# Eight groups of modulation columns summed over partitions by accumulating transfers instead of by TensorE

## The reference, cut to what matters

```python
sh_m, sc_m, gt_m, sh_f, sc_f, gt_f = [m[:, None, :] for m in
    jnp.split(jax.nn.silu(c) @ w_mod[l] + b_mod[l], N_MOD, axis=-1)]
csh_m, csc_m, ... = jnp.split(
    jax.nn.silu(c_ctx) @ w_mod[l] + b_mod[l], N_MOD, axis=-1)
h_lat = modulate(rms_norm_2(x, norm_mix_g[l]), sh_m, sc_m)
h_ctx = modulate(rms_norm_2(y, norm_mix_g[l]), csh_m, csc_m)
```

## Time and profile before

| | us |
|---|---|
| median of 3 runs | 2608.2 |
| lowest and highest | 2608.12 and 2608.32 |
| span of the profiled execution | 2606.1 |

### The profile page before, as it was taken

One profiled execution on the slowest core, in us unless ns is written; L12 is line 12 of the kernel. 1 busy time (PEld: TensorE's weight loads), 2 busy tenths in 40 slices (PEclk: granted clock), 3 DMA queues, 4 the chain that ended last, 5 costly groups with the idle time before them and its releaser, 6 DMA issues.

```text
span 2606.1 us, 35655 instructions
## 1 busy us (share of the span) xinstructions
PE 2588.4 (99%) x13302; PEld 2184.3 (84%) x13302; DVE 1841.0 (71%) x3324; ACT 1367.4 (52%) x2620; POOL 176.2 (7%) x232
## 2 busy tenths in 40 slices
PE   8999999999999999999999999999999999999999
PEld 7999889888888888888888898888788888888887
DVE  5677665677799999666877775667767665555555
ACT  5445565655545445465767565555544444444443
POOL 1011100022100000000011100000001111000000
PEclk9999999999999999999999999999999999999999
DMA  8796655589988888866787765544578887666664
GB/s 271 236 298 183 191 172 173 181 281 286 285 287 271 275 285 267 285 194 198 237 250 233 242 179 147 161 136 148 163 233 254 253 256 226 185 193 192 187 193 161
DMA packets 313724, 576.67 MB, mean 221 GB/s; under 512 B 30012, under 2 KB 38496, under 8 KB 313424
## 3 DMA queue, kind: packets, MB, share of 16 engines
q1 hardware_dynamic: 295824, 558.11, 68.1%
q0 software_dynamic: 17552, 16.22, 3.1%
q10 hardware_dynamic: 176, 0.07, 0.0%
HBM read 568.02 MB, written 2.10 MB: 219 GB/s over the span
## 4 chain that ended last, share of the span: by engine, by line
PE 97%; DVE 1%; ACT 1%; issue 0%; DMA 0%; ACTq 0%; DVEq 0%
PE ps L1825 27%; PE ps L1827 26%; PE ps L1826 26%; PE ps L1814 3%; PE ps L1815 3%; PE ps L1816 3%; PE ps L1758 2%; PE ps L1913 1%; PE ps L1883 1%; PE ps L1902 1%; DVE wlo L2465 0%; PE ps L2028 0%; DVE tl L2511 0%; PE ps L2045 0%; PE ps L2017 0%
## 5 line engine op out<-in xcount | busy, mean ns | idle before, releaser
L2465 DVE TENSOR_TENSOR wlo<-raw,whi 128x512 fp32r<-128x512 f32 x1712 | 1098.6, 687 | 525.5 <-ACT whi L2132 522.8
L2132 ACT ACTIVATE whi<-raw 128x512 fp32r<-128x512 f32 x1712 | 982.2, 624 | 808.2 <-PE ps L1827 516.6
L1825 PE MATMUL ps<-whi,th 128*128 128x512 f32 (+1 forms) x3124 | 1231.7, 394 | 2.2 <-ACT hA L2326 1.0
L1827 PE MATMUL ps<-whi,tl 128*128 128x512 f32 (+1 forms) x3124 | 1211.4, 388 | 0.0
L1826 PE MATMUL ps<-wlo,th 128*128 128x512 f32 (+1 forms) x3124 | 1210.2, 387 | 0.0
L1825 PEld LDWEIGHTS ps<-whi,th 128*128 128x128 f32 x3124 | 586.9, 188 | 122.0 <-issue 5.1
L1827 PEld LDWEIGHTS ps<-whi,tl 128*128 128x128 f32 x3124 | 586.5, 188 | 121.8
L1826 PEld LDWEIGHTS ps<-wlo,th 128*128 128x128 f32 x3124 | 587.3, 188 | 115.7 <-issue 1.0
L2483 DVE SCALAR_TENSOR_TENSOR acc<-raw,silc,acc 128x512 f32<-128x512 f32 x480 | 344.1, 747 | 9.5 <-DMA raw<-in_w_mod 4.9
L1814 PE MATMUL ps<-th,whi 128*128 128x256 f32 x640 | 186.1, 291 | 2.2 <-DVE wlo L2465 2.2
L1816 PE MATMUL ps<-tl,whi 128*128 128x256 f32 x640 | 181.6, 284 | 0.0
(11 more groups left out here) (337 smaller groups left out, 1347.7 us busy)
## 6 DMA issues: line engine op xcount, KB each, us to landing
raw<-in_w_in SPq DMA_DIRECT2D x231, 512.0 KB, 4.0
raw<-in_w_down SPq DMA_DIRECT2D x216, 512.0 KB, 4.5
raw<-in_w_mod SPq DMA_DIRECT2D x192, 512.0 KB, 4.5
raw<-in_w_gate_up SPq DMA_DIRECT2D x176, 512.0 KB, 3.7
raw<-in_w_up SPq DMA_DIRECT2D x128, 512.0 KB, 4.7
raw<-in_w_out SPq DMA_DIRECT2D x64, 512.0 KB, 3.9
raw<-in_xattn_wkv SPq DMA_DIRECT2D x16, 512.0 KB, 3.4
raw<-in_w_in SPq DMA_DIRECT2D x16, 268.0 KB, 3.7
```

The costliest lines, as they stand in the source:

```text
L1825: pe.matmul(p, xh, wh[:, c, c0:n], start=a and (form != "both" or tb == 0), stop=False, skip_group_check=True)
L1827: ins = pe.matmul(p, xl, wh[:, c, c0:n], start=False, stop=z, skip_group_check=True)
L2132: self.e.activation(t.his[g % NHI][:, n * c:n * c + n], t.raws[j % NRAW][:, n * c:n * c + n], ACT.Copy).then_inc(*s.hi.up((g, c)))
L2465: self.e.tensor_tensor(t.los[j % NRAW][:, at], t.raws[j % NRAW][:, at], t.his[g % NHI][:, at].bitcast(F), ALU.subtract).then_inc(*s.lo.up( ...
```

## The change

The branch for one vector in `mod_sum` is now taken for all groups. For groups 0 to 7 each of the seven folds is two transfers, one for each accumulator; the next pair waits for both. Then four transfers scatter the latents' row onto `mod` and four the context's row onto `modx`; each set waits for the same set of the group before. `mod_total` and `mod_turn` are gone on PE, ACT and DVE. `modx` is filled with the bias at the start, in the place of `bmc`. The accumulators of a group are free for group j+2 when their scatters have landed, not when PE has turned them.

```diff
     def mod_sum(self, j, vs):
         for _ in range(LOOK):
             yield
-        if len(vs) == 1:
-            rows = 64
-            while rows:
-                self.mod_fold(j, vs[0], rows)
-                yield
-                rows //= 2
-            self.mod_scatter(j, vs[0])
-            self.acc_after[vs[0]], self.acc_late[vs[0]] = [(self.s.mcolf, j)], False
-            return
-        while not self.side_quiet():
+        rows = 64
+        while rows:
+            self.mod_fold(j, vs, rows)
             yield
-        bank = self.side().take()
-        self.mod_total(j, vs, bank)
...
-        self.mod_turn(j, vs, bank)
-        bank.give((self.s.mcol, j), *([(self.s.mcolx, j)] if len(vs) > 1 else []))
+            rows //= 2
+        self.mod_scatter(j, vs)
         for v in vs:
-            self.acc_after[v], self.acc_late[v] = [(self.s.mtt, j)], False
+            self.acc_after[v], self.acc_late[v] = [(self.s.mcolx if v > 1 else self.s.mcolf, j)], False
...
-    def mod_fold(self, j, v, rows):
+    def mod_fold(self, j, vs, rows):
         t, s, po = self.t, self.s, self.e
         if rows == 64:
-            self.wait_all([self.mod_end(j, 7, [v])])
+            self.wait_all([self.mod_end(j, 7, vs)])
         else:
             self.wait_ge(*s.fold.at((j, 2 * rows)))
-        po.dma_start(t.acc[v][0:rows, :], t.acc[v][rows:2 * rows, :], accum_op=ALU.add).then_inc(*s.fold.up((j, rows), 16))
+        for v in vs:
+            po.dma_start(t.acc[v][0:rows, :], t.acc[v][rows:2 * rows, :], accum_op=ALU.add).then_inc(
+                *s.fold.up((j, rows) if v == vs[-1] else (j, rows, v), 16))
...
         self.scattered = j
+        if len(vs) > 1:
+            if j:
+                self.wait_ge(*s.mcolx.at(j - 1))
+            for a in range(4):
+                po.dma_start(t.modx[:, 4 * j + a:4 * j + a + 1], t.acc[vs[1]][0:1, 128 * a:128 * a + 128], accum_op=ALU.add).then_inc(
+                    *s.mcolx.up(j if a == 3 else (j, a), 16))
...
-        dv.tensor_copy(t.mod[:, 32:96], e[:, 288:352]).then_inc(*s.cols.up("mod"))
-        dv.tensor_copy(t.bmc[:, :], e[:, 256:352]).then_inc(*s.cols.up("bmc"))
+        dv.tensor_copy(t.mod[:, :], e[:, 256:352]).then_inc(*s.cols.up("mod_own"))
+        dv.tensor_copy(t.modx[:, :], e[:, 256:288]).then_inc(*s.cols.up("mod"))
```

More of the change, by code:

```diff
@@ L95, in __init__ @@
             new("hi_made"), new("lo_made"), new("chunk_multiplied"), new("first_rows_multiplied"), new("mod_added"))
-        self.msum, self.mrow, self.mtt, self.mcol, self.mcolx = (
-            new("mod_summed"), new("mod_row"), new("mod_turned"), new("mod_column"), new("mod_column_ctx"))
-        self.fold, self.mcolf = new("mod_folded"), new("mod_scattered")
+        self.fold, self.mcolf, self.mcolx = new("mod_folded"), new("mod_scattered"), new("mod_scattered_ctx")
         self.ld_id, self.ld_gain, self.ld_rest, self.ld_c, self.ld_late = (
@@ L286, in __init__ @@
             small("hT", [2, 32]), small("kcT", [32]), small("ssp", [2, 4]), small("st", [16]), small("sm", [96]))
-        self.dec, self.sink, self.ln4, self.bmc, self.sm2 = (
-            small("dec", [4, 12]), small("sink", [8]), small("ln4", [8]), small("bmc", [96]), small("sm2", [8]))
+        self.dec, self.sink, self.ln4, self.sm2 = (
+            small("dec", [4, 12]), small("sink", [8]), small("ln4", [8]), small("sm2", [8]))
         self.hK, self.hJ = sb("hK", z, [2, 512]), sb("hJ", r_s + 11264, [2, 128])
@@ L531, in mod_cols @@
     def mod_cols(self, j0, j1):
-        return [(self.s.mcol if j < 8 else self.s.mcolf, j) for j in range(j0, j1)]
+        return [(self.s.mcolf, j) for j in range(j0, j1)]
     def mods_until(self, j1):
@@ L1472, in run @@
         self.g_after, self.lb_after, self.z_free = list(free_z), list(ho.end), free_z
-        self.fh_after = free_z + [(s.mtt, 7)]
+        self.fh_after = free_z + [(s.mcolx, 7)]
         fin = [(s.fn, ("fin", 3, 1))]
@@ L1747, in mod_scatter @@
         for a in range(4):
-            po.dma_start(t.mod[:, 4 * j + a:4 * j + a + 1], t.acc[v][0:1, 128 * a:128 * a + 128], accum_op=ALU.add).then_inc(
+            po.dma_start(t.mod[:, 4 * j + a:4 * j + a + 1], t.acc[vs[0]][0:1, 128 * a:128 * a + 128], accum_op=ALU.add).then_inc(
                 *s.mcolf.up(j if a == 3 else (j, a), 16))
         self.scattered = j
+        if len(vs) > 1:
[4 more added lines that the diff above has]
+                    *s.mcolx.up(j if a == 3 else (j, a), 16))
 class Tensor(Program):
@@ L1834, in idle_products @@
             self.e.matmul(bank.tile[:, :], t.ident[:, :], t.mskt[:, 0:512], start=True, stop=True, skip_group_check=True)
[L1836 to L1853, removed]
     def turn_piece(self, name, j, xp, here, bank, op, g, sh, gtok):
@@ L2146, in roots_next @@
         self.e.preload_act_table_set("sqrt_and_others")
[L2148 to L2153, removed]
     def turn_scale(self, name, i, src, landed, rs, v):
@@ L2485, in mod_add @@
                 ins.then_inc(*s.mod.up((j, kc, c, v)))
[L2487 to L2492, removed]
-            dv.tensor_tensor(t.modx[:, 4 * j:4 * j + 4], e[:, 128:256:32], t.bmc[:, 4 * j:4 * j + 4], ALU.add).then_inc(*s.mcolx.up(j))
     def root(self, name, dst, n, after):
```

12 lines of the change are left out of this document (3 added, 9 removed).

## The result

The changed kernel takes **2616.8 us** in the median of five runs (2611.8 to 2625.0), the kernel before 2608.2 (2608.1 to 2608.4). The ratio is 1.0040, 95% interval 1.0029 to 1.0051. It is slower, by 8.6 us in the median, where the forecast was 5.9 us faster; the time lies outside the range. The execution whose trace follows is the fastest of the five: 2611.8 us, a span of 2609.9 against 2606.1 before, 3.8 us longer.

The account below looks back on a forecast made before the run. The prediction took PE as the bound, DVE close behind, POOL idle. From 2608.2 us, 8.6 us less for matmuls taken away and 2.7 us more for PE's waits made -5.9 us: 2602.3 us, range 2599.0 to 2613.0.

Parts of the forecast that it names:

- Matmuls taken away, 8.6 us: On PE, groups 0 to 7: without ones and transposes 1.08 us less a group, 8.6 us for eight.
- the DMA engines fill up: Rival, chance 0.18 (with rounds of 5.5 to 5.7): DMA share limited to 0.95, groups take 46.2 us, 2607.2 us.
- +0.7 a round, 38.0 us for seven: POOL's folds: the second transfer of a pair adds 0.49 us of descriptors and 0.2 for the later landing.
- the landing of the last scatter: End of a group's chain on POOL: 2.6 us after its descriptors, 48.1 us after the group's last addition.
- 1.2, then 0.9 a group: DVE's first additions: 1.2 us late at group 2, 0.9 more each group, 7.7 at group 7 with 2 added.
- sign of being wrong in the rounds: DVE's first additions of groups 2 to 7: waits absent or above 5 us each would show the rounds wrong.
- the 2.6 us a group: DVE's free time in the stretch from 742 to 1062 us: 18.4 us over seven groups.
- The lead of 5 us: DVE's low parts are 5 us ahead of PE, so PE waits 7.7 - 5 = 2.7 us in all.
- The end of the stretch: After group 7: scatters landed at 1111, the context's fourth load near 1116, in time for its use.
- the cover: Slack of the context's fourth load behind the last scatters: some 9 us; without it each us would be a us.
- VectorE keeping POOL from its descriptors: A skill page's rule: VectorE operations taking both ports stop GpSimd's descriptor writes; would lengthen rounds; no row showed it.
- POOL becomes the bound: Rival, chance 0.18: rounds of 5.8 us, POOL needs 48.1 us a group, PE waits 18.3 us, 2617.9 us.

Follow-up runs that it names:

- no_sum: The kernel before without its sum over partitions for groups 0 to 7 (no ones, transposes or ACT copies, no transfers instead): 2599.5 us, ratio 0.9966.
- no_ctx_scatter: The changed kernel without the four context scatters of each group: 2610.2 us, ratio 1.0006 to the kernel before.
- four_sets: The changed kernel with four pairs of accumulators instead of two, all transfers kept: 2619.2 us, ratio 1.0039 to the kernel before.
- traffic: The kernel before, sums on PE kept, plus the same folds and scatters on spare memory, sums thrown away: 2639.6 us, ratio 1.0123.

## Why the prediction was wrong, point by point

**Matmuls taken away, 8.6 us: right.** `no_sum` gave 8.7.

**Traffic beside the weights is harmless, and the rival "the DMA engines fill up" is out:** PE without a pause at shares of 0.93, 0.95 and 0.96.

**"+0.7 a round, 38.0 us for seven": wrong, and with it the landing of the last scatter; these are the terms that turned the sign.** The waits for landings were right, 165.5 / 41 = 4.04 us against 3.98 from the earlier trace rows: the seven of a group take 28.7 us in the mean, where the prediction had 27.6 and 1.4 for the later of two. Too small was POOL's own part. The step took the second transfer of a pair at the 0.49 us of a plain load, though the earlier trace rows has 0.79 for this very operation. I had 7 x 1.28 = 9.0 us of descriptors; measured are 1.7 for the first pair and six times 1.58, 11.2. The eight scatters take 7.2 us, as predicted. With 0.4 us for a wait for DVE and the loads in between that makes 47.5 us a group, against 45.5. Too small was also the time to the last landing, 2.6 us behind the scatters' descriptors: it took 4.0 to 4.4 at groups 0 to 6. The 4.6 of the earlier trace rows is the median of all four scatters; the last ones of groups 11 to 15, looked at by themselves, landed 2.7 to 4.0 us after their descriptors. From group 0's last addition to its scatters' landing it is 51.3 us against 48.1. Put into the prediction's own sum, 2.2 us more of descriptors and 1.5 more of landing make DVE 51.8 - 46.9 = 4.9 us late at group 2, 4.9 + 5 x 2.9 + 2 = 21.4 at group 7, PE waits 16.4, and the sum is +7.8: 2616.0 us, slower and no longer faster. That this lies so near to the median is in part luck, for PE's waits and the clock share it otherwise, as follows.

**"1.2, then 0.9 a group": wrong in form.** The lateness was to grow steadily to 7.7 us at group 7. DVE waited 5.9 us at group 2 already and 8.0 at group 5, 26.1 in all; waits above 5 us were the prediction's own sign of being wrong in the rounds. Of group 2's wait 3.2 us are the late landing, and 2 come from DVE: it stood ready 44.9 us after group 0's last addition, not 46.9. Chains vary by 7 us within an execution, and what counts with two sets is each chain, not the mean. The other side of it I had missed too: between waits DVE wins back its lead, with the 2.6 us a group that the prediction itself had read off. An account with a lead of 6 us at the start and 2.6 won back each group: at group 2, 6 - 5.9 leaves 0.1; at group 3, 2.7 - 5.9 makes PE wait 3.2; at group 4, 2.6 - 1.7 leaves 0.9; at group 5, 3.5 - 8.0 makes it wait 4.5; at group 6, 2.6 - 3.7, 1.1. The trace has 0.4, 2.7 and 5.3 at groups 2, 3 and 5, in sum 8.4 against 8.8. It is an estimate: in `no_ctx_scatter` a wait of 6.1 us at group 2 already made PE pause for 2.7, where the account has 0.1.

**The lead of 5 us:** a little low, 6 to 6.7 measured. By itself this would have made the changed kernel faster than forecast.

**The clock: missing from the prediction.** It had PE wait 2.7 us in small pieces, and put nothing on the clock. The pause of 5.7 us costs 3 us more than itself, and that is about what separates the profiled execution from no change.

**The end of the stretch: right here, but thinner than said.** Group 7's scatters started at 1115.1, later than the 1111 at which they were to have landed, and the context's last load was issued behind them. ACT took up the context at 1135.6 and DVE the columns at 1138.4 with no wait. `four_sets` (12 us of wait) and `traffic` (35 us) show that beyond the cover each us is at least a us, as the prediction said; the clock's surcharge comes on top.

**VectorE keeping POOL from its descriptors: not seen.** A pair takes POOL 1.6 us with DVE busy 298 of 325 us, and 1.57 to 1.59 in `traffic` from 1147 to 1154, where DVE does nothing.

**The rival "POOL becomes the bound"** gave 2617.9 us, and the median is 2616.8. Its mechanism is the one seen, with rounds of 5.9 us where it had 5.8, and 47.5 us a group where it had 48.1; its reason, later landings, is not the main one seen. But its sum is not confirmed by that: it had PE wait 18.3 us, and the trace shows 8.4 and a slow clock. The median execution is 5 us longer than the profiled one, at a mean clock of 0.996 to 0.998; that speaks for longer or more pauses, and of such an execution there is no trace. That part stays open.

## What to carry to other kernels

When work moves from a busy engine to a chain of transfers on an idle one, price the issue of the exact transfer and not that of a similar one, and the landing of the last one and not the median, and compare the slowest link of the chain, not its mean, with the buffers that wait for it. If the resource is only late and not full, more buffers and fewer, wider transfers bring back the gain, but first ask what else stands in that queue at the end. And a pause of TensorE can be worth more than its length: here one of 3.8 us was not, and those of 5.7 us and more were, by up to 3 us.

## What was not expected of the hardware

The granted clock fell to half with every stretch of 5.7 us and more without a matmul (seven traces), and PE ran at half clock for another 3.1 to 6.2 us after it, no longer after 33.1 us than after 5.7; it did not fall with 3.8 us. A fold's landing depends little on its size (POOL waits 4.04 us, 3.87 with half the bytes, 4.69 for twice the row at a higher DMA share), but much on company: 1.4 to 1.6 us when no weights flow. Transfers of 128 single numbers take POOL 0.9 us of descriptors each, and POOL takes up further transfers before these are done: a pair of folds queued behind eight of them shows 4.6 us in its row, of which 1.7 are its own.
